# High and low tokens of the feeds' up and value projections in one product of 512 columns

## What is computed

```python
def conv_gated_ffn(x, w_up, conv_w, conv_b, w_down):          # w_up 1024 x 5632, w_down 2816 x 1024
    h = x @ w_up
    h = lax.conv_general_dilated(h, conv_w[:, None, :], ..., padding=[(CONV_WIDTH - 1, 0)], ...) + conv_b
    gate, val = jnp.split(h, 2, axis=-1)
    return (jax.nn.silu(gate) * val) @ w_down

# second block, per layer                                      w_ffn_in 1024 x 5632, w_ffn_out 2816 x 1024
    gt, up = jnp.split(h @ w_ffn_in[l], 2, axis=-1)
    x = x + (jax.nn.silu(gt) * up) @ w_ffn_out[l]
```

## Time and profile before

| | |
|---|---|
| median of 3 runs | 2276.24 us |
| profiled execution | 2277.58 us |
| its span (first to last instruction) | 2275.8 us |
| mean granted TensorE clock | 0.972 |
| PE / PEld busy | 95% / 88% |
| DVE / ACT / POOL busy | 42% / 47% / 66% |
| `w_lo` on GpSimd (L348) | 602 instructions, 1463.0 us |
| `w_hi` on ScalarE (L339) | 602 instructions, 635.7 us |
| transfers | 333.05 MB, mean 146 GB/s |

### The profile page before, as it was taken

The page is one execution under the profiler, slowest core; times in us unless marked ns, Lnnn a source line. Parts: engine busy times, 40 slices in busy tenths (PEclk is TensorE's granted clock), DMA queues, the critical chain, the costliest instruction groups (busy, mean ns, idle before and its releaser), DMA issues.

```text
span 2275.8 us, 35984 instructions
## 1 busy us (share of the span) xinstructions
PE 2163.2 (95%) x15336; PEld 2001.3 (88%) x15336; DVE 955.9 (42%) x1484; ACT 1073.0 (47%) x1517; POOL 1498.6 (66%) x632
## 2 busy tenths in 40 slices
PE   8989989899969899999999899998999999999998
PEld 7789978799959888989999899898889899998998
DVE  4353256442375537477112211456374681123112
ACT  4555555555545352255444444473441454544444
POOL 6679877698846234356778688663243566786886
PEclk9999999999989999999999999999999999999999
DMA  8345544355524113134445455442131344454553
GB/s 338 132 146 204 185 139 161 117 180 187 184 84 147 60 71 106 64 128 167 151 164 185 148 185 185 156 145 90 56 112 56 130 148 149 157 182 150 184 185 133
DMA packets 47183, 333.05 MB, mean 146 GB/s; under 512 B 5168, under 2 KB 5552, under 8 KB 7856
## 3 DMA queue, kind: packets, MB, share of 16 engines
q1 hardware_dynamic: 47024, 330.76, 41.9%
HBM read 329.69 MB, written 1.05 MB: 145 GB/s over the span
## 4 chain that ended last, share of the span: by engine, by line
PE 62%; DVE 8%; issue 1%; ACT 1%; POOL 0%; DVEq 0%; ACTq 0%
PE bank L147 14%; PE bank L149 14%; PE bank L148 14%; PE y L147 2%; PE y L149 2%; PE y L148 2%; PE bank L1749 2%; PE bank L1748 1%; PE bank L1739 1%; DVE conv L1384 1%; PE bank L1672 1%; PE bank L1794 1%; PE bank L1791 1%; PE bank L1774 1%; DVE sq L1583 1%
## 5 line engine op out<-in xcount | busy, mean ns | idle before, releaser
L348 POOL TENSOR_TENSOR w_lo<-w_raw,w_hi 128x1024 fp32r<-128x1024 f32 x602 | 1463.0, 2437 | 759.7 <-ACT w_hi L339 759.6
L339 ACT ACTIVATE w_hi<-w_raw 128x1024 fp32r<-128x1024 f32 x602 | 635.7, 1059 | 1009.4 <-PE bank L149 838.9
L147 PE MATMUL bank<-x_hi,w_hi 128*128 128x256 f32 x2960 | 876.6, 296 | 21.6 <-POOL w_lo L348 17.1
L148 PE MATMUL bank<-x_lo,w_hi 128*128 128x256 f32 x2960 | 848.4, 287 | 0.0
L149 PE MATMUL bank<-x_hi,w_lo 128*128 128x256 f32 x2960 | 848.3, 287 | 0.0
L147 PEld LDWEIGHTS bank<-x_hi,w_hi 128*128 128x128 f32 x2960 | 579.1, 196 | 44.9 <-issue 24.4
L148 PEld LDWEIGHTS bank<-x_lo,w_hi 128*128 128x128 f32 x2960 | 579.0, 196 | 10.5 <-issue 8.6
L149 PEld LDWEIGHTS bank<-x_hi,w_lo 128*128 128x128 f32 x2960 | 578.4, 195 | 0.0
L876 DVE SCALAR_TENSOR_TENSOR conv<-bank,par_sb,conv 128x254 f32<-128x254 f32 (+1 forms) x176 | 76.8, 478 | 240.1 <-ACT conv L864 238.6
L1246 DVE TENSOR_TENSOR hid_lo<-hid,hid_hi 128x512 fp32r<-128x512 f32 x22 | 45.1, 2048 | 241.2 <-ACT hid_hi L1241 241.2
L147 PE MATMUL y<-w_hi,hid_hi 128*128 128x512 f32 x352 | 139.9, 397 | 3.3 <-DVE hid_lo L898 3.3
(11 more groups left out here) (397 smaller groups left out, 3243.6 us busy)
## 6 DMA issues: line engine op xcount, KB each, us to landing
w_raw<-w SPq DMA_DIRECT2D x300, 1024.0 KB, 4.8
ln_rows<-ln_rows SPq DMA_DIRECT2D x4, 1024.0 KB, 7.2
mem_tok<-mem SPq DMA_DIRECT2D x2, 1024.0 KB, 4.9
const_sb<-const SPq DMA_DIRECT2D x1, 1536.0 KB, 9.3
par_sb<-par SPq DMA_DIRECT2D x2, 553.5 KB, 10.7
xn<-xT SPq DMA_DIRECT2D x1, 1024.0 KB, 4.9
w_raw<-w SPq DMA_DIRECT2D x2, 512.0 KB, 5.4
x_tok<-x SPq DMA_DIRECT2D x1, 1024.0 KB, 7.2
```

The lines of the kernel that those rows point to most:

```text
L147: pe.matmul(out, lhs[0], rhs[0], start=start, stop=False, skip_group_check=skip)
L148: pe.matmul(out, lhs[0], rhs[1], start=False, stop=False, skip_group_check=skip)
L339: act.activation(self.hi[:, h % HALVES, :], self.raw[:, n % RAWS, i * HW:(i + 1) * HW], ACT.Copy).then_inc(*sig.up("high", h))
L348: pool.tensor_tensor(self.lo[:, h % HALVES, :], self.raw[:, n % RAWS, i * HW:(i + 1) * HW], self.hi[:, h % HALVES, :].bitcast(F32), ALU.su ...
```

## The change

In the feeds, the first 20 of the 22 up (gate) and value units become wide. `x_hi` and `x_lo` now lie behind each other in one tensor `x_pair` (their size is the same), so `w_hi` can take both in one product of 512 columns, 256 high tokens and 256 low tokens, with two results side by side. `w_lo` on `x_hi` stays a product of 256 columns, summed onto the first result. A tile of 128 features now fills a whole bank, a unit two (`wide0` is banks 0 and 1, `wide1` banks 2 and 3), and units alternate between two places instead of rotating over four.

The two results have to be added. At the end of a wide unit ScalarE copies the second one to SBUF (`second_copy`, L2601), VectorE adds it onto the first in PSUM (`second_join`, L2605), and then the unit's work goes on as before from the first. In the first block's feed and in the gate units, ScalarE waits for the join inside its own queue. Units 20 and 21 (up10 and val10, gate 10 and value 10) keep the three products.

```diff
+def wide_passes(pe, out, w, x, start, stop):
+    pe.matmul(out, w[0], x, start=start, stop=False, skip_group_check=True)
+    return pe.matmul(out[:, 0, :], w[1], x[:, 0, :], start=False, stop=stop, skip_group_check=True)
...
         def conv_unit(n, i, val):
-            bank = net.bank[n % 4]
+            wide, bank = net.wide[n % 2], net.bank[2 * (n % 2)]
...
             def act(act):
                 act.wait_ge(*sig.at("product", u.last))
+                if u.wide:
+                    net.second_copy(act, wide, "first", l, n)
+                    act.wait_ge(*sig.at("joined", "first", l, n))
                 if n >= 3:
...
             def dve(dve):
+                if u.wide:
+                    net.second_join(dve, wide, "first", l, n)
                 dve.wait_ge(*sig.at("affine", l, n))
...
-            need = [("tapped", l, n - 4)] if n >= 4 else list(net.feed_need(l, n))
+            need = [("tapped", l, n - 2)] if n >= 2 else []
...
         def gate_unit(i):
+                if u.wide:
+                    net.second_copy(act, wide, "second", l, 2 * i)
+                    act.wait_ge(*sig.at("joined", "second", l, 2 * i))
...
-                     [("silu", "second", l, i - 2)] if i >= 2 else [], ready=ready if i == 0 else None, act=act, dve=dve)
+                     [("silu", "second", l, i - 1)] if i else [], ready=ready if i == 0 else None, act=act, dve=dve, wide=i < 10)
...
         def value_unit(i):
             def act(act):
+                if u.wide:
+                    act.wait_ge(*sig.at("product", u.last))
+                    net.second_copy(act, wide, "second", l, 2 * i + 1)
...
             def dve(dve):
+                if u.wide:
+                    net.second_join(dve, wide, "second", l, 2 * i + 1)
+                    dve.wait_ge(*sig.at("joined", "second", l, 2 * i + 1))
...
-                     [("hid", "second", l, i - 2)] if i >= 2 else [], act=act, dve=dve)
+                     [("hid", "second", l, i - 1)] if i else [], act=act, dve=dve, wide=i < 10)
...
+    def second_copy(self, act, wide, block, l, n):
+        if n >= 2:
+            act.wait_ge(*self.sig.at("joined", block, l, n - 2))
+        act.activation(self.second[block][:, n % 2, :, :], wide[:, :, 1, :], ACT.Copy).then_inc(*self.sig.up("second", block, l, n))
+
+    def second_join(self, dve, wide, block, l, n):
+        dve.wait_ge(*self.sig.at("second", block, l, n))
+        dve.tensor_tensor(wide[:, :, 0, :], wide[:, :, 0, :], self.second[block][:, n % 2, :, :], ALU.add
+                          ).then_inc(*self.sig.up("joined", block, l, n))
```

More of the change, by code:

```diff
@@ L287, with __init__ @@
 class Unit:
-    def __init__(self, chunks, layout, x, out, need=(), ready=None, act=None, dve=None, pool=None, more=False, early=None):
+    def __init__(self, chunks, layout, x, out, need=(), ready=None, act=None, dve=None, pool=None, more=False, early=None, wide=False):
+        self.wide = wide
         self.chunks, self.layout, self.x, self.out, self.need = chunks, layout, x, out, need
@@ L396, in pe @@
                         u.ready(pe, k)
-                    mm = passes(pe, u.out[:, j * T:(j + 1) * T], [v[:, k, :] for v in w], [v[:, k, :] for v in u.x],
-                                k == 0, k == KD - 1)
+                    if u.wide:
+                        mm = wide_passes(pe, u.out[:, j, :, :], [v[:, k, :] for v in w], u.x[2][:, :, k, :], k == 0, k == KD - 1)
+                    else:
+                        mm = passes(pe, u.out[:, j * T:(j + 1) * T], [v[:, k, :] for v in w], [v[:, k, :] for v in u.x[0:2]],
+                                    k == 0, k == KD - 1)
             elif u.layout == "tokens":
@@ L402, in pe @@
                 for tt in range(TT):
-                    mm = passes(pe, u.out[tt], [v[:, k, tt * P:(tt + 1) * P] for v in u.x], [v[:, part, :] for v in w],
+                    mm = passes(pe, u.out[tt], [v[:, k, tt * P:(tt + 1) * P] for v in u.x[0:2]], [v[:, part, :] for v in w],
                                 k == 0, k == KD - 1)
@@ L888, in dve @@
                     dve.tensor_tensor(hid, g, cb, ALU.mult).then_inc(*sig.up("hid", l, i))
-            need = [("tapped", l, n - 4)] if n >= 4 else list(net.feed_need(l, n))
-            u = Unit([(chunk(l, f"{'val' if val else 'up'}{i}"), 2)], "features", net.xs, bank, need,
-                     ready=ready if n == 0 else None, act=act, dve=dve)
+            need = [("tapped", l, n - 2)] if n >= 2 else []
+            u = Unit([(chunk(l, f"{'val' if val else 'up'}{i}"), 2)], "features", net.xs, wide if n < 20 else bank, need,
+                     ready=ready if n == 0 else None, act=act, dve=dve, wide=n < 20)
             return u
@@ L1262, in dve @@
             def dve(dve):
+                if u.wide:
+                    net.second_join(dve, wide, "second", l, 2 * i)
                 if i:
                     low(dve, i - 1)
-            u = Unit([(chunk(l, f"fin{i}"), 2)], "features", net.xs, bank,
-                     [("silu", "second", l, i - 2)] if i >= 2 else [], ready=ready if i == 0 else None, act=act, dve=dve)
+            u = Unit([(chunk(l, f"fin{i}"), 2)], "features", net.xs, wide if i < 10 else bank,
+                     [("silu", "second", l, i - 1)] if i else [], ready=ready if i == 0 else None, act=act, dve=dve, wide=i < 10)
             return u
         def value_unit(i):
-            bank = net.bank[(2 * i + 1) % 4]
+            wide, bank = net.wide[1], net.bank[2]
+            view = wide[:, :, 0, :] if i < 10 else bank[:, :].rearrange("p (i t) -> p i t", i=2)
             def act(act):
+                if u.wide:
+                    act.wait_ge(*sig.at("product", u.last))
+                    net.second_copy(act, wide, "second", l, 2 * i + 1)
                 if i == 10:
@@ L1277, in dve @@
             def dve(dve):
-                dve.wait_ge(*sig.at("product", u.last))
+                if u.wide:
+                    net.second_join(dve, wide, "second", l, 2 * i + 1)
+                    dve.wait_ge(*sig.at("joined", "second", l, 2 * i + 1))
+                else:
+                    dve.wait_ge(*sig.at("product", u.last))
                 dve.wait_ge(*sig.at("silu", "second", l, i))
@@ L2397, in __init__ @@
         self.const = area.take("const_sb", [P, NCC2])
-        self.xs = [area.take(f"x_{n}", [P, KD, T], F32R)[:, :, :] for n in ("hi", "lo")]
+        pair = area.take("x_pair", [P, 2, KD, T], F32R)
+        self.xs = [pair[:, 0, :, :], pair[:, 1, :, :], pair[:, :, :, :]]
         self.xtok = area.take("x_tok", [P, TT, D])
@@ L2406, in __init__ @@
         self.y = banks(nc, "y", 4, 4)
+        self.wide = [banks(nc, f"wide{i}", 2 * i, 2)[:, :].rearrange("p (i s t) -> p i s t", i=2, s=2) for i in range(2)]
         self.first_memory(area.rest())
@@ L2469, in first_memory @@
         self.hs1 = [feed.take(f"hid_{n}", [P, 6, T], F32R)[:, :, :] for n in ("hi", "lo")]
+        self.second = {"first": feed.take("second1", [P, 2, 2, T])}
         self.rot1 = [banks(nc, "rot0", 2), banks(nc, "rot1", 3)]
@@ L2527, in second_memory @@
         self.xn2 = place("xn2", 32, [P, TT, D])
+        self.second["second"] = place("second2", 72, [P, 2, 2, T])
         m["gain"] = place("final_gain", 16, [P, D])
@@ L2565, in norm_ready @@
         return ready
-    def feed_need(self, l, n):
-        return ()
+    def second_copy(self, act, wide, block, l, n):
[6 more added lines that the diff above has]
+                          ).then_inc(*self.sig.up("joined", block, l, n))
     def down_need(self, l):
```

13 lines of the change are left out of this document (6 added, 7 removed).

## The result

The changed kernel takes 2313.73 us (median of 4 runs, 2311.59 to 2316.84), the kernel before 2276.09 us beside it. The ratio is 1.0166 (95% interval 1.0148 to 1.0183): 37.6 us slower, where the forecast was 2311 us. The profiled execution has a span of 2313.1 us at a mean granted clock of 0.964 (2275.8 us and 0.972 before).

The account below looks back on a forecast made before the run. TensorE was taken to set the pace in the feeds, with the chain to `hid_lo` ending nearly as late. Products -8.0, pauses +47.0, today's waits -3.9 gave +35.1 us: 2311 us forecast, range 2288 to 2343.

Parts of the forecast that it names:

- The order of the views: Whole kernel: read busy shares, then a window in a feed, then TensorE's timeline, then TensorE's waits in the feeds.
- the walk: End of a first-block up unit, timed step by step: `hid_lo` ends at 7.84 us, TensorE loses 2.61 us.
- the 0.16 us between the two starts: First block's feed: `w_lo` starts at 4.89 us, `hid_lo` comes at 5.05, 0.16 us too late.
- The total of +35.1 us: Whole kernel: -8.0 for products, +47.0 for pauses, -3.9 for today's waits; the span goes from 2275.8 to 2310.9 us.
- a clock below 1.00 behind the pauses: Windows behind the first block's pauses: a lower granted clock there was named as a sign of the forecast being wrong.
- 18 pauses of 2.61 us: First block, downs behind wide up units 1 to 9, two layers: TensorE waits for `hid_lo`, +47.0 us, less 3.9.
- then the pattern starts anew: First block's feeds: GpSimd and VectorE catch up in each pause, so it repeats at 9 downs a layer, 18.
- Rival B: Behind the first block's pauses TensorE gets its lower clock, 1.3 to 1.7 us each; at all 18, 2334 to 2342; chance 0.15.
- The products, -8.0: All four feeds, 80 wide units: a step takes 353.1 ns for 359.4, 0.10 us a unit, -8.0 us.
- Second block untouched by pauses: Second block's feeds: `hid_lo` ends near 4.1 us, where it ends today too; no wait there.
- bank waits 0: Units waiting for `tapped` two units back: 0 us, and 0.1 to 0.3 us four times if the join is longer.

Follow-up runs that it names:

- experiment 2: The changed kernel plus a ScalarE copy between `hid_hi` and the next `w_hi` in the first block: 2277.04 us with 512 columns, 2276.35 us with 128.
- run 22: Not a run's label but a count, "run 22 times": the 128-column ScalarE copy added to the changed kernel; that kernel takes 2276.35 us, ratio 0.9995.
- three_products: The changed kernel with the product of 512 columns split into two of 256, copy, join and banks as changed: 2320.59 us, ratio 1.0195.

## Why the prediction was right, and where it wasn't

The order of the views and the mechanism held: the gain of the products is small, the chain to `hid_lo` was nearly critical, and `hid_lo` meets `w_lo`. Every time of the walk is within 0.06 us of the trace, and experiment 2 shows that the 0.16 us between the two starts (0.19 measured) is what the 37 us hang on.

The total of +35.1 us (+37.3 by the spans) is right partly by luck, because two wrong terms cancel; and one of the signs that the prediction named for being wrong, a clock below 1.00 behind the pauses, did come.

- **18 pauses of 2.61 us, +43.1 net.** It was twelve, at 2.45 + 0.1 us, and six short ones: net +32.4. The step that failed is "then the pattern starts anew" for the first three downs of a layer. There GpSimd also has instructions of the last norm for `x_tok` (at 140, 153 and 165 us) and works nearly without a gap up to 190 us, so that `hid_lo` meets an instruction near its end, not its start (at 165.14 us, 0.4 us ahead of it: `hid_lo` 0.95 us).
- **The clock, 0 in the forecast, +12.1.** Rival B was given 0.15 and came at eight of the twelve long pauses, 1.5 us each. Its price was right and its chance too low. The prediction took it from one pause of 2.2 us that left the clock at 1.00. The trace before has eight pauses of TensorE of 2.04 to 2.22 us, and behind five of them the lower level was granted, behind one of the same 2.22 us too. Windows behind one of 2.04 us and behind that one:

```profile
775.70:779.10 3.40, 3.40 (x19) 3.40 (x20) 0.93 (x2) 0.00 (x0) 0.00 (x0) 0.64 0.64 265
1701.90:1705.30 3.40, 3.40 (x17) 3.40 (x18) 1.84 (x3) 0.60 (x1) 0.00 (x0) 0.54 0.68 275
```

  The Trainium skill ("TensorE: Matmul & The Clock Gate", section "HAM oscillation — how this bites in real kernels") tells of a kernel in which TensorE waited some 3 to 5 us between groups of products and each group started at the lower clock. The pauses here are shorter; the lower clock came behind eight of the twelve of 2.3 to 2.4 us, and behind none of 1.4 us.
- **The products, -8.0.** Inside the cuts the first block's 32 wide units gave 4.0 us, 0.12 us each for the 0.10 said, and the second block's 32 gave 5.2 us, 0.16 us each. For all 80 that makes an estimate of -11.
- **Second block untouched by pauses, bank waits 0:** right. Its `hid_lo` even became shorter (0.69 for 2.00 us), starting 0.09 us before a `w_lo` ended.
- **Elsewhere, 0 in the forecast:** +2.6 us, of the size by which unchanged stretches differ from kernel to kernel.

## What to carry to other kernels

Before lengthening a chain, look at who waits for its end and by how much, and not only at the busy shares: here 1.1 us of room in a chain decided, while the engines that got the work were half idle. Where VectorE and GpSimd both read two operands from SBUF, the order of their starts can cost the one who comes second nearly the whole instruction of the other (here `hid_lo` took 2.72 us for 0.68 behind a `w_lo` of 2.36); so keep a critical VectorE instruction out of the moment in which GpSimd is released, or shift that moment, even by adding a small instruction. Merging products of equal weights saves only the fixed part per product, here 6 to 13 ns of 359. And a rival is priced from every row that bears on it: the one pause that the earlier trace rows shows with a whole clock behind it had a twin of the same length with the lower one.

## What the hardware showed that was not expected

- An added ScalarE instruction of 128 columns, run 22 times, made the kernel 37 us faster.
- Pauses of TensorE of nearly one length (2.27 to 2.40 us idle) in the same surroundings brought the clock down in eight cases and left it in four (2.29 us each), in the same order in both layers; pauses of 1.38 us never did. The place isn't what decides: with the second block narrow, nine of the twelve downs were at the lower clock, down 3 of the first layer among them, and in `three_products` seven, behind pauses of 2.18 us and in another order in each layer. No run tells what decides.
- In the second block the wide step is 347 ns in every other pair of units and 353 in the rest (periods of 16.68 and 16.85 us, before 17.09); in the first it is 347 ns in four pairs of the sixteen. The timeline of TensorE in such a pair:

```profile
1358.86 0.40 PE L154 MATMUL wide<-x_pair,w_hi 128*128 128x512 f32 x1
1359.09 0.28 PE L155 MATMUL wide<-x_pair,w_lo 128*128 128x256 f32 x1
1359.21 0.39 PE L154 MATMUL wide<-x_pair,w_hi 128*128 128x512 f32 x1
...
1360.94 0.40 PE L154 MATMUL wide<-x_pair,w_hi 128*128 128x512 f32 x1
```

  Six steps in 2.08 us, 347 ns each. No run tells why.
- Stretches that the kernels have (nearly) in common varied between their profiled executions: from the first block's first down 10 to the next down 0 (norms, a mixer and four units) 146.1 to 153.2 us, from the second down 10 to the second block's down 0 660.8 to 666.3 us. That is as much as the smaller effects above, so differences of 5 us between two versions rest on the feeds' own lengths, not on the totals.
